# Context rows' keys and values of a neighbourhood attention, moved from its own layer to the experts' stage

## The reference, cut to what matters

```python
def second_block(x, c, ctx, ...):
    for i in range(2):
        h = x * (1.0 + sc1) + sh1
        hc = ctx * (1.0 + sc1c) + sh1c
        if i == 0:
            y, yc = retention_mixer(h, hc, ...)
        else:
            y, yc = neighbourhood_mixer(h, hc, nat_w_in, nat_w_o, nat_rpb, False)
        x = layer_norm(DN_ALPHA * x + g1 * y, ...)
        h = x * (1.0 + sc2) + sh2
        x = layer_norm(DN_ALPHA * x + g2 * sq_relu_mlp(h, ...), ...)
        if i == 0:
            ctx = layer_norm(DN_ALPHA * ctx + g1c * yc, ...)
            hc = ctx * (1.0 + sc2c) + sh2c
            ctx = layer_norm(DN_ALPHA * ctx + g2c * sq_relu_mlp(hc, ...), ...)
    return x

def neighbourhood_mixer(h_lat, h_ctx, w_in, w_o, rpb, ctx_out):
    p = h_lat @ w_in                       # queries, keys, values of the 256 rows
    pc = (h_ctx @ w_in[:, d:])             # keys and values of the context
    # 32 heads of width 32: each row attends its window and all context rows
```

## Time and profile before

| | |
|---|---|
| time, median of 3 runs (lowest to highest) | 2381.99 us (2381.11 to 2387.13) |
| the profiled execution | 2390.99 us |
| its span | 2389.3 us |
| PE busy | 2178.5 us, 91% |
| DVE busy | 1376.1 us, 58% |
| ACT busy | 639.1 us, 27% |
| POOL busy | 111.1 us, 5% |
| moved by DMA | 711.73 MB, mean 298 GB/s |
| chain that ended last | PE 66%, DVE 16%, DMA 13%, ACT 3%, issue 2% |

### The profile page before, as it was taken

The page is one execution under the profiler, slowest core; times in us unless marked ns, Lnnn a source line. Parts: engine busy times, 40 slices in busy tenths (PEclk is TensorE's granted clock), DMA queues, the critical chain, the costliest instruction groups (busy, mean ns, idle before and its releaser), DMA issues.

```text
span 2389.3 us, 40011 instructions
## 1 busy us (share of the span) xinstructions
PE 2178.5 (91%) x16396; PEld 1515.2 (63%) x16396; DVE 1376.1 (58%) x2656; ACT 639.1 (27%) x806; POOL 111.1 (5%) x195
## 2 busy tenths in 40 slices
PE   6998989998898998988998899899989999998998
PEld 5887843454545444445545555777769898876987
DVE  2455554634453443565545546866678776678866
ACT  1111120121222221211111111444433334444332
POOL 0000010000000000000000000000000000000000
PEclk8999989999999999999999999999989999999999
DMA  9778879999999999999999999444445533234651
GB/s 379 293 293 336 314 289 377 410 420 365 419 419 419 417 419 419 415 417 419 404 419 419 411 403 387 164 154 150 152 143 202 191 124 124 98 132 140 213 183 64
DMA packets 111243, 711.73 MB, mean 298 GB/s; under 512 B 12480, under 2 KB 13136, under 8 KB 36128
## 3 DMA queue, kind: packets, MB, share of 16 engines
q1 hardware_dynamic: 85904, 616.93, 65.4%
q0 software_dynamic: 25168, 92.38, 10.2%
HBM read 705.06 MB, written 4.19 MB: 297 GB/s over the span
## 4 chain that ended last, share of the span: by engine, by line
PE 66%; DVE 16%; DMA 13%; ACT 3%; issue 2%; SPq 0%; DVEq 0%; ACTq 0%
PE bank L312 17%; PE bank L2268 7%; PE bank L2249 6%; PE bank L1981 4%; PE bank L2019 4%; DMA hT<-in_panels_e 3%; PE bank L1644 3%; DMA cst<-in_panels_e 2%; PE bank L1494 2%; DMA ring<-in_units_a 2%; PE bank L2354 2%; DMA hid<-in_panels_e 2%; PE bank L2134 2%; PE bank L1996 2%; PE bank L2123 1%
## 5 line engine op out<-in xcount | busy, mean ns | idle before, releaser
L312 PE MATMUL bank<-hid,scratch 128*32 128x512 f32 x1008 | 309.9, 612 | 6.3 <-DMA hT<-in_panels_e 3.7
L312 PE MATMUL bank<-hT,scratch 128*32 128x512 f32 x976 | 300.3, 603 | 11.3 <-DMA hT<-in_panels_e 9.5
L1258 ACT CAST chi<-craw 128x1024 fp32r<-128x1024 f32 x128 | 133.7, 1045 | 548.2 <-DMA craw<-in_panels_m 214.3
L3272 DVE TENSOR_TENSOR clo<-craw,chi 128x1024 fp32r<-128x1024 f32 x128 | 156.0, 1222 | 155.1 <-ACT chi L1258 154.0
L312 PE MATMUL bank<-yacc,scratch 128*32 128x512 f32 x648 | 179.2, 610 | 4.6 <-DMA diag_gtmp<-in_panels_e 4.6
L312 PE MATMUL bank<-diag_gtmp,scratch 128*32 128x512 f32 x648 | 179.1, 603 | 2.9 <-DMA hid<-in_panels_e 1.5
L312 PE MATMUL bank<-rows,scratch 128*32 128x512 f32 x632 | 171.4, 601 | 7.2 <-DMA cst<-in_panels_e 7.2
L312 PE MATMUL bank<-cst,scratch 128*32 128x512 f32 x632 | 173.6, 603 | 2.7 <-DMA yacc<-in_panels_e 2.7
L1981 PE MATMUL bank<-cT_hi,chi 128*128 128x256 f32 x384 | 112.8, 294 | 17.8 <-DVE crot_lo L3246 6.3
L312 PEld LDWEIGHTS bank<-hT,scratch 128*32 128x32 f32 x976 | 70.2, 111 | 62.9 <-issue 62.2
L1981 PE MATMUL bank<-cT_lo,chi 128*128 128x256 f32 x384 | 109.9, 286 | 0.0
(11 more groups left out here) (670 smaller groups left out, 5595.6 us busy)
## 6 DMA issues: line engine op xcount, KB each, us to landing
hid<-in_panels_e SPq DMA_DIRECT2D x96, 1024.0 KB, 12.9
hT<-in_panels_e SPq DMA_DIRECT2D x94, 1024.0 KB, 13.7
ring<-in_units_a SPq DMA_DIRECT2D x88, 1024.0 KB, 7.5
ring<-in_panels_m SPq DMA_DIRECT2D x64, 1024.0 KB, 5.1
yacc<-in_panels_e SPq DMA_DIRECT2D x48, 1024.0 KB, 11.9
diag_gtmp<-in_panels_e SPq DMA_DIRECT2D x48, 1024.0 KB, 14.2
rows<-in_panels_e SPq DMA_DIRECT2D x47, 1024.0 KB, 13.1
cst<-in_panels_e SPq DMA_DIRECT2D x47, 1024.0 KB, 13.1
```

Source lines behind the costliest of these rows:

```text
L312: m = self.pe.matmul(b[s:s + STRIP, :], lhs(k)[:, s:s + STRIP], v, start=(first and k == 0), stop=(k == KT - 1))
L1258: act.copy(chi[:, h % 2, :], context_raw(h)).then_inc(cx_hi, 1)
L3272: tt(context_lower(h), context_raw(h), chi[:, h % 2, :], ALU.subtract).then_inc(cx_lo, 1)
```

## The change

The work table gets twenty pieces at its end: statistics and normalisation of the context rows after their last layer, two feature pieces that transpose, scale and split them, and for each of the four head groups two "nk" and two "nv" pieces, the attention's keys (PE, the "hid" form) and values (24 products of 256 columns a piece). Their 16 weight units are the halves of `in_units_n`, loaded by POOL. DVE copies each finished pair into one of three places, and POOL writes it to `kept_nat`, eight writes of 128 x 512 floats. In the attention POOL reads them back (`keys_back`, `values_back`), between its loads of the bias, and `scores` waits for them at the first step of a group. The products of the context rows there go, as does the transposing and splitting of their features in the first MLP, and their statistics and normalisation in the retention layer. Keys of own rows are two 256-column products in one bank, emptied by one copy. A value step holds one product where it held two. In the last group the attention's sums stand in steps 0 and 1 where they stood in 1 and 2. SP's wait for the context's units before the retention's loads keeps its number. POOL's loop of bias loads is written out.

```diff
@@ context_pieces
+    work += [("stat", 1, 0), ("norm", 1, 0), ("feat", 2, 0), ("feat", 2, 1)]
+    work += [(kind, q, part) for q in range(NAT_GROUPS // 2) for kind in ("nk", "nv") for part in range(2)]
...
+MLP_FIRST = 16 * RET_HEADS
+KV_FIRST = MLP_FIRST + 64
+KEPT = NAT_GROUPS
@@ context_unit
+    if h >= KV_FIRST:
+        i, half = divmod(h - KV_FIRST, 2)
+        return 3 * (i // 2) + 2 * (i % 2), half
@@ SP
-            sp.wait_ge(cx_used, c_units - 4)
+            sp.wait_ge(cx_used, KV_FIRST - 4)
@@ POOL
+            def keep(j):
+                pool.wait_ge(cx_free, kept_fills[j])
+                pool.dma_start(nat_kv[j], kept_rows[j % 3]).then_inc(cx_out, 16)
...
+                kept_unit = h - KV_FIRST - 5
+                if kept_unit >= 0 and kept_unit % 2 == 0:
+                    keep(kept_unit // 2)
...
+            def keys_back(q):
+                pool.dma_start(nk[:, q % 2, :, SEQ:2 * SEQ], nat_kv[2 * q].rearrange("p (a n) -> p a n", a=2))\
+                    .then_inc(cx_back, 16)
+            def values_back(q):
+                pool.dma_start(nv[:, q % 2, 2:4, :], nat_kv[2 * q + 1].rearrange("p (a n) -> p a n", a=2))\
+                    .then_inc(cx_out, 16)
...
+                    for half in range(2, 2 * NAT_GROUPS):
+                        pool.wait_ge(score_used, half - 1)
+                        load_bias(half)
+                        if half in (7, 11):
+                            keys_back((half + 1) // 4)
+                            values_back((half + 1) // 4)
@@ PE, context_piece
-                opens = p.part % 2 == 0 if p.kind in ("out", "hid", "sum") else p.kind == "feat" or p.part == 0
+                opens = p.part % 2 == 0 if p.kind in ("out", "hid", "sum", "nk", "nv") else p.kind == "feat" or p.part == 0
...
+                if p.kind == "nv":
+                    w = [v.rearrange("p (k n) -> p k n", k=4) for v in parts]
+                    for t in range(XT):
+                        for k in range(4):
+                            for c, (x, y) in enumerate(three):
+                                m = pe.matmul(cbank[t][:, 0:SEQ], features_of(p, 4 * p.part + k)[x][:, t * P:t * P + P], w[y][:, k, :],
+                                              start=(p.part == k == c == 0), stop=(p.part == 1 and k == 3 and c == 2))
+                        if p.part and t == 0:
+                            m.then_inc(cx_full, 1)
+                    m.then_inc(cx_used, 1)
@@ PE, attention
             def scores(q, s):
+                if s == 0 and q != 1:
+                    later = max(q - 1, 0)
+                    pe.wait_ge(cx_back, 32 * RET_HEADS + 16 * (2 + later))
+                    pe.wait_ge(cx_out, kept_before + 16 * (KEPT + 2 + later))
...
-                    if s in (1, 2):
-                        sums_part(11 + s, second)
+                    if s < 2:
+                        sums_part(12 + s, second)
...
-                if s == 0:
-                    key_part(n, second)
-                elif s == 1:
-                    if not second:
-                        held.append(N.open())
-                    query_part(n + 1, held[-1], second)
-                else:
-                    if not second:
-                        held.append(N.open())
-                    value_part(n + 2, held[-1], 2 * (s - 2) + second)
+                if s < 2:
+                    if not second:
+                        held.append(N.open())
+                    columns_part(n + s, held[-1], second)
+                elif not second:
+                    value_part(n + 2, s - 2)
...
-            base = F.c.n - 4
-            w = nat_parts(0)
-            halves_product(w, cols, 1, base)
             from_dve.get()
             turn_features(0)
-            first, last_m = halves_product(w, cols, 0, base + 4)
+            first, last_m = halves_product(nat_parts(0), cols, 0, F.c.n - 4)
@@ DVE
+                if p.kind in ("nk", "nv") and p.part:
+                    j = 2 * p.head + (p.kind == "nv")
+                    if j >= 3:
+                        dve.wait_ge(cx_out, kept_before + 16 * (j - 2))
+                    for u in range(2):
+                        copy(kept_rows[j % 3][:, SEQ * u:SEQ * u + SEQ], tile(u)[:, 0:SEQ]).then_inc(cx_free, 1)
```

More of the change, by code:

```diff
@@ L711, in program @@
         kv = nc.dram_tensor("kept_kv", (RET_HEADS, P, 2 * SEQ + XT * 512), F32, kind="Internal").ap()
+        kept_fills = [p.fills + 2 for q in range(KEPT // 2) for kind in ("nk", "nv")
+                      for p in c_pieces if (p.kind, p.head, p.part) == (kind, q, 1)]
+        nat_kv = nc.dram_tensor("kept_nat", (KEPT, P, 2 * SEQ), F32, kind="Internal").ap()
+        kept_before = 32 * RET_HEADS
         tiles_free = sem("tiles_free")
@@ L816, in banks_of, with kept_features, features_of @@
         def banks_of(p):
-            return bank[4:6] if p.kind == "sum" and p.part >= 2 and p.head == 7 else cbank
+            return bank[4:6] if (p.kind, p.head) == ("nv", KEPT // 2 - 1) else cbank
+        def kept_features(k):
+            if k < 4:
+                return crot_hi[:, k, :], crot_lo[:, k, :]
+            return cg_rows[:, k - 4, :], tok_low[:, k // 2 - 2, SEQ * (k % 2):SEQ * (k % 2) + SEQ]
+        def features_of(p, k):
+            return kept_features(k) if p.kind in ("nk", "nv") else (cT_hi[:, k, :], cT_lo[:, k, :])
+        kept_rows = [cgate[:, 0:2 * SEQ], cgate[:, 2 * SEQ:4 * SEQ], cq.rearrange("p a n -> p (a n)")]
         def context_raw(h):
@@ L2290, in first_hidden, with turn @@
                     lo_units.n += 1
-                def turn(between=lambda c, h: None):
+                def turn():
                     for n in range(4):
@@ L2296, in turn @@
                         for h in range(2):
-                            between(c, h)
                             second(c, h)
@@ L3196, in context_out @@
                         c_step(m)
-                    elif p.part:
+                    elif p.part and p.head == 1:
                         dve.wait_ge(ctx_in, 48)
@@ L3589, in _ @@
                 lower(n)
-                if i == 1:
-                    roots_in((2, 3))
-                    for t in range(XT, 4):
-                        m = ts(tok[:, t, :], tok[:, t, :], mv[:, t, 0:1], rstd[:, t:t + 1], ALU.subtract, ALU.mult)
-                    step(m)
                 scores()
@@ L3739, in _, with first_keys, keys @@
             halves, probs = Count(), Count()
-            def keys(q, u):
+            def first_keys(u):
                 b = N.take(u == 1)
-                N.done(copy(nk[:, q % 2, u, :], b[:, :]))
+                N.done(copy(nk[:, 0, u, 0:SEQ], b[:, 0:SEQ]))
+            def keys(q):
+                b = N.take(True)
+                N.done(copy(nk[:, q % 2, :, 0:SEQ], b[:, :].rearrange("p (g n) -> p g n", g=2)))
             def queries(q):
```

180 lines of the change are left out of this document (79 added, 101 removed).

## The result

| | before | after |
|---|---|---|
| median | 2384.56 us (4 runs, 2381.11 to 2390.51) | 2424.18 us (4 runs, 2422.45 to 2428.16) |
| ratio | | 1.0146, 95% interval 1.0121 to 1.0171 |
| span of the profiled execution | 2389.3 us | 2420.8 us |

The two medians differ by 39.6 us; the ratio, 1.0146, is 35 us, and the repeat further down (a1) gives 33. I take 35. The two spans differ by 31.5 us, and the trace splits them at the gather that each expert turn makes once (L1902 before, L1950 after). The stretch of ten turns between the gathers took 1011.3 us and takes 1069.6: +58.3, after a start 2.5 us earlier. From the last gather to the end it was 923.9 us and is 899.6: -24.3. So the last part gave nearly what was expected (some of the added products also stand behind the last gather), and the experts' stage cost more.

The account below looks back on a forecast made before the run. Transfers (1020 us) and PE (1002) nearly both bound the experts' stage, with PE the larger after the change; PE bounds the attention. +42 - 30 - 1 = +11 us on the median of 2381.99 gave 2393 us, range 2367 to 2413.

Parts of the forecast that it names:

- The last part: Last layer: removing context products, transposes and keys was to give -30 us, between -24 and -40.
- Value steps: Attention in the last layer: one product instead of two, 10.46 to 8.25 us a step, -10.6 us in all.
- the key step of the second group: Attention in the last layer: the step of 16.1 us was to fall to 12.4, -3.7 us.
- The experts' stage: 454 to 1490 us of the trace: added pieces were to lengthen it by 42 us, between +25 and +65.
- Products and transposes: Experts' stage, PE: 16 added pieces at 2.83 us, +45, and transposes of context features, +2.
- New waits for other engines: Experts' stage: PE standing where bank pairs close and open together, and for the new normalisation, +18 us, between 0 and 36.
- Nothing by itself: Experts' stage: splitting 16 weight units on DVE, 1.22 us each, was to cost nothing; without idle cover 20 us.
- rival D: Experts' stage clock: filling PE's gaps gives back at most 31 us of half-speed time, 2362 us; chance 0.07.
- Panel waits: Experts' stage: PE's 34 us of waits for panels; 11 us was left over PE's need after the change.
- B: Experts' stage stays bound by transfers, new PE work fills panel waits: +25 - 31 = -6, 2376 us; chance 0.20.
- C: Experts' stage bound by transfers and attention falling at PE's pace: -18, 2364 us; chance 0.14.
- E: Experts' stage: no panel wait shrinks, since later buffers start later loads: +34, 2416 us; chance 0.11.

Follow-up runs that it names:

- a1: The changed kernel measured once more, unaltered, beside the others of its group: 2425.03 us, 1.0137 of the kernel before.
- b1: The changed kernel without the pieces added to the experts' stage, leaving the changed last part: 2359.81 us, 0.986 of the kernel before.
- a2: The changed kernel with the same pieces, ordered so no pair of banks opens where the one before closed: 2423.46 us, 1.0139.
- b2: The kernel before, its own pieces placed so 61 pairs of banks open where the one before closed, instead of 16: 2486.29 us, 1.0411.
- c4: The kernel before with 16 "hid" pieces making their products twice and 10.5 MB of extra transfers, old order: 2441.44 us, 1.0211.
- c3: The kernel before, each of 16 pair-opening "hid" pieces making its 24 products twice, no bytes added: 2424.83 us, 1.0142.
- f1: The kernel before, each of eight pair-opening "q" and "k" pieces making its 24 products twice, all in the first half: 2393.58 us, 1.0026.
- c2: The changed kernel with its pieces spread 1 to 1 between turns of three and two shares, instead of 4 to 1: 2429.98 us, 1.0171.
- d1: The kernel before with its own pieces spread 2 to 1 between turns of three and two shares: 2395.19 us, 1.0028.
- c1: The changed kernel with its pieces spread 2 to 1 between turns of three and two shares, instead of 4 to 1: 2406.36 us, 1.0063.
- a3: The kernel before, its pieces ordered so no pair of banks opens where the one before closed: 2385.56 us, 0.9983.
- a4: The changed kernel with each added key and value piece making 6 products of 24, loads, evictions and writes kept: 2418.76 us, 1.0118.

## Why the prediction was wrong

**The last part** was forecast at -30 us and -1 for the retention layer, and b1 measured -33. Value steps took 8.24 us (forecast 8.3) and the idle at the entrance 4.88 (4.87). One step was read too well: the key step of the second group took 13.73 us (forecast 12.4, under 13 as a sign) and gave 2.4 us, not 3.7. (In the sum, the two value products of the lead-in are 2 x 2.83 = 5.7, not 5.8; nothing hangs on it.)

**The experts' stage** was forecast at +42 and took +58 between the traces, where the tail behind the last gather is not counted. By the terms of the sum:

- Products and transposes, forecast +47. Between the gathers stand 264 products of 256 columns more (31 us at 118 ns), 48 of 512 (11 us at 231 ns) and 16 transposes (2 us): 44; the last pieces come later. The term was right.
- New waits for other engines, forecast +18. PE's idle without the panel waits was 98.2 - 34.5 = 64 us and is 100.5 - 3.6 = 97: +33. This term was mis-sized. The neighbours came as counted, seven from "hid" to "hid" and seven from "sum" to "hid", but they cost 22.9 and 12.1 us where 7 x 2.43 = 17.0 and 7 x 0.88 = 6.2 were the prices. The prices of the earlier trace rows were those of a DVE that stood ready; in a point with two pieces it has the next unit's split, and often an expert bank, ahead of the eviction. The waits for `clo` grew from 4.2 to 15.9 us, and the forecast had put them at nothing ("Nothing by itself"), because DVE has idle time in the stage as a whole. a2 shows that taking the neighbours out doesn't help: then the split is waited for instead, and the panels.
- The clock, forecast 0 in the sum. PE's busy time grew by 56 us, 12 more than the products; between traces of the same pieces it differs by up to 5. The earlier trace rows already held stands of this length, but I carried the clock only as a gain (rival D), never as a cost of new stands. b2 shows it alone: 27 us more for the same instructions. The Trainium skill, "TensorE: Matmul & The Clock Gate", section on HAM oscillation, says idle gaps put the engine at half its clock. By that rule a new stand costs its length and then the slow pace behind it. The trace agrees for the stand of 5.58 us: 0.63 granted in the 4 us after it.
- Panel waits, 34 us left to be 11: they fell to 4, the only term that helped. 44 + 33 + 12 - 31 = 58.

**The step that failed** is thus "PE needs 1002 + 45 + 2 + 18 = 1067 us", 65 more than before. Between the gathers and without its panel waits PE needed 1011.3 - 34.5 = 977 us and needs 1069.6 - 3.6 = 1066: 89 more. The rule that took the larger of the two limits and a little more held for this kernel; the time stood 4 us over PE's need.

**The same rule fails for c4**, which adds products and bytes in the old order: it forecasts 1002 + 45 = 1047 against 1045, so about +20; measured +50. It treats 34 us of panel waits as one pool, but they lie 25 in the first half and 10 in the second. c3 and f1 show what that means: 45 us of products in the second half cost 36 there, 22.6 in the first half cost 5. It did not spoil the forecast of the changed kernel, whose pieces moved into both halves and used up the waits of both: 24.6 and 9.9 us before, 3.6 and 0 after.

The rivals: B and C needed a stage that stays bound by transfers; it fell to 380 GB/s in the stretch from 955 us. E came nearest in its number (2416, +34), but by luck, since its reason was wrong: the panel waits did shrink. Expectations failed in the experiments too, above all that neighbours (a2) or points with two pieces (c2, d1) set the cost. What is shown is that the order of pieces moves the time by -19 us (c1) and +98 us (b2). Which placement costs how much is not settled: the same number of full points, and nearly the same number of neighbours, gave 2406 and 2431 us.

No version beat the kernel before by more than can be told: 0.9983 for a3 is the best.

## What to carry to other kernels

When more pieces go into the same gaps, price the wait for a bank or a weight with everything that stands ahead of it on the evicting engine, and add the slower clock after each long stand. An engine that is idle for half of a stage can still be late at the one point where it is waited for.

Slack has a place. Before summing a bound over a stage, split its waits by turns, and count for each moved piece only the waits of the turns that receive it. Where the slack lies in other turns than the added work, added work and added bytes can cost nearly their sum, as in c4.

## What the runs showed of the hardware

- The same 6353 PE instructions were busy 913 us at a granted clock of 0.97 and 940 us at 0.95 (b2): stands of a few microseconds cost again in the pace after them.
- The reverse in one turn (a4): 180 products fewer, 21 us at the usual 118 ns, took only 13 us off PE's busy time, because the granted clock fell from 0.96 to 0.88 in the emptier turn.
- The 419 GB/s of single turns came back: the fullest turn of each of the 20 traces moved 417 to 421 GB/s. 10.5 MB more cost 14 to 18 us, against 25 at that rate; that part of them found room in stretches that weren't full is likely, but not shown. "DMA: Bandwidth & Descriptors" of the Trainium skill, section on where 436 GB/s comes from, gives about 358 for such transfers; the measurement decides for 419.
